# Attention in an encoder block: V as the stationary operand with two heads side by side in the array's columns, the two local score groups interleaved on row halves, and no transposes of the mixed heads

## The reference

```
# local heads: 8 query heads of 64, 2 kv groups of 4 heads; query block of 128
s = q @ k.T * 64**-0.5 - slope[h] * |distance|     # keys: 16 meta + blocks n-1, n, n+1
m = max(max(s), sink[h]); p = exp(s - m)
y_a = (p / (sum(p) + exp(sink[h] - m))) @ v
# latent (MLA) heads: 8 heads, q and k of 96, v of 64, all 1040 keys
y_b = softmax(q @ k.T * 96**-0.5) @ v
h = x + concat(y_a, y_b) @ w_out
# then RMSNorm and a top-4-of-32 mixture of experts, added to h
```

## Time and profile before

| | |
|---|---|
| median of 3 runs | 2566.9 us (2562.52 to 2570.47) |
| the profiled execution's own time | 2575.11 us |
| its span in the trace | 2573.4 us |
| mean granted TensorE clock | 0.945 of full speed |
| attend, by the trace | about 252.5 to 885 us |

### The profile page before, as it was taken

The page is one execution under the profiler, slowest core; times in us unless marked ns, Lnnn a source line. Parts: engine busy times, 40 slices in busy tenths (PEclk is TensorE's granted clock), DMA queues, the critical chain, the costliest instruction groups (busy, mean ns, idle before and its releaser), DMA issues.

```text
span 2573.4 us, 36097 instructions
## 1 busy us (share of the span) xinstructions
PE 2425.0 (94%) x15012; PEld 1858.4 (72%) x15012; DVE 749.6 (29%) x2121; ACT 452.7 (18%) x1120; POOL 224.3 (9%) x251
## 2 busy tenths in 40 slices
PE   7998999999999774799999999999999999999996
PEld 3554767777777561777888788788787878787875
DVE  4555433543444255111122122122121212121211
ACT  2333332332333130101111111111111111111110
POOL 0000000000000005011121111121100000000000
PEclk9999898998999755899999999999999999999998
DMA  3000300000000222976777788788889888888873
GB/s 144 24 2 21 125 17 1 17 17 17 17 17 9 66 93 82 386 256 225 264 271 279 264 290 292 277 292 298 321 305 326 306 325 305 326 304 325 304 267 83
DMA packets 199046, 486.41 MB, mean 189 GB/s; under 512 B 15137, under 2 KB 17313, under 8 KB 198417
## 3 DMA queue, kind: packets, MB, share of 16 engines
q1 hardware_dynamic: 176864, 442.85, 46.5%
q0 software_dynamic: 16320, 38.27, 6.4%
q10 hardware_dynamic: 5696, 2.95, 0.4%
HBM read 452.51 MB, written 38.21 MB: 191 GB/s over the span
## 4 chain that ended last, share of the span: by engine, by line
PE 59%; DMA 1%; POOL 0%; issue 0%; POOLq 0%; ACT 0%; ACTq 0%
PE gu_bank L1677 37%; PE ya_bank L1691 17%; PE yb_bank L1704 2%; PE xa_bank L1647 1%; PE xb_bank L1655 0%; DMA x_rows<-ffn_rows,tab 0%; DMA tab_b<-slot_table 0%; POOL x_rows L1445 0%; POOL sums L1488 0%; ACT y_rows L1562 0%; POOLq L1468 0%; POOL tab_b L1452 0%; ACTq L1580 0%; POOLq L1448 0%; POOLq L1452 0%
## 5 line engine op out<-in xcount | busy, mean ns | idle before, releaser
L1677 PEld LDWEIGHTS gu_bank<-xT,ring 128*128 128x128 f32 x8192 | 965.1, 191 | 15.5 <-issue 15.5
L1677 PE MATMUL gu_bank<-xT,ring 128*128 128x128 f32 (+10 forms) x8192 | 968.5, 281 | 0.7 <-issue 0.7
L1691 PE MATMUL ya_bank<-ring,hidden 128*128 128x512 f32 x1024 | 446.2, 594 | 0.0
L1605 DVE TENSOR_SCALAR g_in<-gu_bank,bias_cur 128x128 f32<-128x128 f32 (+10 forms) x256 | 91.9, 359 | 1192.2 <-PE gu_bank L1677 1192.2
L1691 PEld LDWEIGHTS ya_bank<-ring,hidden 128*128 128x128 f32 x1024 | 192.0, 190 | 230.0 <-issue 225.5
L1556 ACT ACTIVATE sig<-g_in 128x128 f32<-128x128 f32 (+10 forms) x256 | 81.3, 317 | 875.8 <-DVE g_in L1605 875.8
L484 PE MATMUL proj_bank<-w_in_sb,normT 128*128 128x512 f32 (+3 forms) x432 | 149.8, 501 | 9.8 <-DVE w_in_sb L369 8.9
L867 PE MATMUL score_bank<-mla_kT,mla_qT 96*128 96x512 f32 x256 | 140.9, 678 | 0.0
L1488 POOL DMA_INDIRECT sums<-y_rows,tab x32 | 51.7, 1616 | 963.1 <-ACT y_rows L1562 963.1
L484 PEld LDWEIGHTS proj_bank<-w_in_sb,normT 128*128 128x128 f32 (+1 forms) x432 | 70.9, 182 | 78.4 <-issue 65.6
L907 PE MATMUL mla_bank<-mla_v,probsT 128*128 128x64 f32 x1024 | 121.4, 272 | 0.0
(11 more groups left out here) (240 smaller groups left out, 1863.4 us busy)
## 6 DMA issues: line engine op xcount, KB each, us to landing
ring<-in_w_gate SPq DMA_DIRECT2D x64, 2048.0 KB, 12.3
ring<-in_w_up SPq DMA_DIRECT2D x64, 2048.0 KB, 10.6
ring<-in_w_down SPq DMA_DIRECT2D x64, 2048.0 KB, 14.2
w_in_sb<-in_w_in SPq DMA_DIRECT2D x8, 592.0 KB, 8.8
xt<-in_x SPq DMA_DIRECT2D x8, 512.0 KB, 3.9
resid<-in_x SPq DMA_DIRECT2D x8, 512.0 KB, 3.6
w_out_sb<-in_w_out SPq DMA_DIRECT2D x1, 4096.0 KB, 16.9
residual<-resid SPq DMA_DIRECT2D x8, 512.0 KB, 2.6
```

The costliest lines, as they stand in the source:

```text
L1605: v.tensor_scalar(g_in[:, f % 2, 0:width], gu_bank[:, f % 2, 0:width], bias_cur[:, f:f + 1], LIMIT, ALU.add, ALU.min).then_inc(g_ready, 1)
L1677: last = nc.tensor.matmul(gu_bank[:, f % 2, i * 256:i * 256 + width], w[:, k, c * P:(c + 1) * P], xT[:, k, 0:width], start=(k == 0), stop= ...
L1691: last = nc.tensor.matmul(ya_bank[:, h, :], hidden[:, k, 0:P], w[:, k % 4, h * 512:(h + 1) * 512], start=(k == 0), stop=(k == FC - 1))
```

## The change

- **Values, MLA heads.** V is now stationary (64 columns) and `probsT` moving (128 columns). The output has head dimensions on the partitions: head 2p on partitions 0 to 63 and head 2p+1 on 64 to 127 of `mla_bank`, and the code alternates between the two (`mla_values`). It works on a pair of heads at once, half of the key blocks in one step and half in the next. `probsT` gets four buffers.
- **Local heads.** A unit is now a pair of heads, one of each kv group: `UNITS = 12`. Its scores alternate between array rows 0 to 63 and 64 to 127 and go to separate banks; its values (`swa_values`) are paired in the columns as above. Its transposes are split between `act_bank` and `dve_bank`.
- **Normalisation.** The output is already transposed, so `mixed` and its eight transposes go away. To scale along the free dimension, TensorE spreads each head's inverse sum over 64 partitions by a matmul with the identity (8 matmuls for MLA in step i = 10, 8 for local heads in step i = 1), ScalarE copies the bank to `inv_wide`, and VectorE multiplies it with the values' bank straight into `mixedT`. The output projection moves from step i = 5 to i = 3.
- **Meta values.** One matmul of 512 columns becomes four of 128.
- **DMAs.** `w_out` comes in three DMAs with its local half reordered. The rows past the end of `sums` are filled from `x` by one DMA instead of zeros by a memset and two.

```diff
@@ attend @@
-    UNITS = MLA_HEADS + SWA_HEADS
+    UNITS = MLA_HEADS + PAIRS
+    EVENTS = MLA_HEADS // 2 + PAIRS
...
-        no_rows = m.sb("no_rows", [P, 2 * D])
-        probsT = m.sb("probsT", [P, 2, DC, P])
-        biased = m.sb("biased", [P, 2, BAND])
+        probsT = m.sb("probsT", [P, 4, DC, P])
+        biased = m.sb("biased", [P, 2, SWA_KV, BAND])
-        mixed = m.sb("mixed", [P, 2 * 512])
+        inv_wide = m.sb("inv_wide", [P, 512])
...
@@ gpsimd @@
-                nc.gpsimd.memset(no_rows[:], 0.0).then_inc(no_rows_set, 1)
-                pool.wait_ge(no_rows_set, 1)
-                for b in range(0, TRASH, 2 * P):
-                    pool.dma_start(io["acc"][SEQ + b:SEQ + b + 2 * P, :].rearrange("(p j) d -> p (j d)", p=P), no_rows[:])\
-                    .then_inc(y_zeroed, 16)
+                pool.dma_start(io["acc"][SEQ:SEQ + TRASH, :].rearrange("(p j) d -> p (j d)", p=P),
+                               io["x"][0, 0:TRASH, :].rearrange("(p j) d -> p (j d)", p=P)).then_inc(y_zeroed, 16)
@@ scalar @@
+                    if i == 10:
+                        if t >= 1:
                             act.wait_ge(swa_mixed, t)
+                        copy_T(("mla", t), inv_wide[:], act_bank[:]).then_inc(act_T_out, 1)
+                    if i == 1 and t >= 1:
+                        act.wait_ge(mla_mixed, t)
+                        copy_T(("swa", t - 1), inv_wide[:], act_bank[:]).then_inc(act_T_out, 1)
@@ vector @@
+                    if i == 1 and t >= 1:
+                        dve.wait_ge(sink_done, t)
+                        link(v.tensor_tensor(swa_inv[:], band_sum[:].rearrange("p (g j) -> p j g", j=PAIRS),
+                                             sink_exp[:].rearrange("p (g j) -> p j g", j=PAIRS), ALU.add))
+                        v.reciprocal(swa_inv[:], swa_inv[:]).then_inc(swa_inverse, 1)
...
+                    if i == 2 and t >= 1:
+                        dve.wait_ge(values_done, t * EVENTS)
+                        dve.wait_ge(act_T_out, at_act["swa", t - 1] + 1)
+                        v.tensor_tensor(mixedT[:, 0:4, :].rearrange("p k q -> p (k q)"), swa_bank[:], inv_wide[:], ALU.mult)\
+                            .then_inc(swa_mixed, 1)
@@ tensor: scores @@
-                        g, pair = divmod(i - MLA_HEADS, PAIRS)
-                        r = slice(g * HD, (g + 1) * HD)
                         for at, key, keys, _, _ in band_parts(t):
-                            last = nc.tensor.matmul(bank[:, at:at + keys], swa_qT[r, pair, cols(t)],
-                                                    swa_kT[r, key:key + keys], start=True, stop=True)
+                            for g in range(SWA_KV):
+                                r = slice(g * HD, (g + 1) * HD)
+                                last = nc.tensor.matmul(bank[:, g * 512 + at:g * 512 + at + keys],
+                                                        swa_qT[r, i - MLA_HEADS, cols(t)],
+                                                        swa_kT[r, key:key + keys], start=True, stop=True)
@@ tensor: values @@
-                        for k in range(DC):
-                            last = nc.tensor.matmul(mla_bank[:, i * VD:(i + 1) * VD], probsT[:, n % 2, k, :],
-                                                    mla_v[:, k, i, :], start=(i == 0 and k == 0), stop=False,
-                                                    skip_group_check=True)
+                    for k in range(4 * half, 4 * half + 4):
+                        for j in range(2):
+                            last = nc.tensor.matmul(mla_bank[j * VD:(j + 1) * VD, pair * P:(pair + 1) * P],
+                                                    mla_v[:, k, 2 * pair + j, :], probsT[:, (n - 1 + j) % 4, k, :],
+                                                    start=(pair == 0 and k == 0), stop=False, skip_group_check=True)
...
+                    for x, (_, _, keys, kt, slot) in enumerate(parts):
+                        for g in range(SWA_KV):
+                            last = nc.tensor.matmul(swa_bank[g * HD:(g + 1) * HD, pair * P:(pair + 1) * P],
                                                     swa_v[0:keys, kt, g * HD:(g + 1) * HD],
+                                                    probsT[0:keys, n % 4, 4 * g + slot, :],
                                                     start=(x == 0), stop=(x == len(parts) - 1))
@@ tensor: inverse sums, out @@
+                        pe.wait_ge(mla_inverse, t + 1)
+                        pe.wait_ge(act_T_out, at_act["mla", t])
+                        for h in range(MLA_HEADS):
+                            p, j = divmod(h, 2)
+                            last = nc.tensor.matmul(act_bank[j * VD:(j + 1) * VD, p * P:(p + 1) * P],
+                                                    mla_inv[:, h:h + 1].to_broadcast([P, VD]), ident[:],
+                                                    start=True, stop=True)
...
-                            for k in range(4):
-                                c = (c0 + k) * P
-                                last = nc.tensor.transpose(bank[:, k * P:(k + 1) * P], mixed[:, c:c + P], ident[:])
```

More of the change, by code:

```diff
@@ L620, in attend @@
         dve_own = m.sem("dve_own_a")
-        fills, act_T, dve_T = [], [], []
-        for n in range(TILES * UNITS + 8):
+        OUT = 3
+        STEPS = TILES * UNITS + OUT + 2
+        fills, act_T = [], []
+        for n in range(STEPS):
             t, i = divmod(n, UNITS)
@@ L777, in _ @@
                 take_meta(0)
-                for n in range(TILES * UNITS + 8):
+                for n in range(STEPS):
                     t, i = divmod(n, UNITS)
-                    if i == 6 and t >= 1:
+                    if i == OUT + 1 and t >= 1:
                         j = at_fill["out", t - 1]
@@ L897, in transpose_probs @@
-                    last.then_inc(dve_T_done, 1)
-                def values(n):
+                        if g == 1 and n:
+                            pe.wait_ge(dve_T_out, n)
+                        if i < MLA_HEADS:
+                            for k in range(4):
+                                last = nc.tensor.transpose(bank[:, k * P:(k + 1) * P],
+                                                           probs[:, n % 2, (4 * g + k) * P:(4 * g + k + 1) * P], ident[:])
+                        else:
+                            for c, _, keys, _, slot in band_parts(t):
+                                last = nc.tensor.transpose(bank[0:keys, slot * P:(slot + 1) * P],
+                                                           probs[:, n % 2, g * 512 + c:g * 512 + c + keys], ident[:])
@@ L900, in values, with mla_values @@
+                        last.then_inc(done, 1)
+                def mla_values(n, half):
                     t, i = divmod(n, UNITS)
-                    pe.wait_ge(dve_T_out, at_dve["unit", n] + 1)
-                    if i < MLA_HEADS:
+                    pair = i // 2
+                    if half == 0:
+                        pe.wait_ge(dve_T_out, n + 1)
                         pe.wait_ge(act_T_out, at_act["unit", n] + 1)
-                        if i == 0 and t >= 1:
+                        if pair == 0 and t >= 1:
@@ new lines, in mla_values, with swa_values @@
+                    if half:
+                        last.then_inc(values_done, 1)
+                def swa_values(n):
+                    t, i = divmod(n, UNITS)
+                    pair = i - MLA_HEADS
+                    pe.wait_ge(dve_T_out, n + 1)
+                    pe.wait_ge(act_T_out, at_act["unit", n] + 1)
+                    if pair == 0:
+                        pe.wait_ge(meta_read, min(t + 2, TILES))
+                    parts = band_parts(t)
+                    for x, (_, _, keys, kt, slot) in enumerate(parts):
+                        for g in range(SWA_KV):
+                            last = nc.tensor.matmul(swa_bank[g * HD:(g + 1) * HD, pair * P:(pair + 1) * P],
@@ L939, in _ @@
                             pe.wait_ge(v_meta_in, 16 * MLA_HEADS)
-                        nc.tensor.matmul(mla_bank[:], meta_pT[:], v_meta[:].rearrange("p h c -> p (h c)"),
-                                         start=False, stop=True, skip_group_check=True).then_inc(mla_done, 1)
-                    if i == 3 and t >= 1:
-                        pe.wait_ge(swa_mixed, t)
-                        pe.wait_ge(mla_mixed, t)
-                        for bank, out, done, key, c0 in ((act_bank, act_T_out, act_T_done, at_act["mixed", t - 1], 0),
-                                                         (dve_bank, dve_T_out, dve_T_done, at_dve["mixed", t - 1], 4)):
-                            pe.wait_ge(out, key)
-                            for k in range(4):
-                                c = (c0 + k) * P
-                                last = nc.tensor.transpose(bank[:, k * P:(k + 1) * P], mixed[:, c:c + P], ident[:])
-                            last.then_inc(done, 1)
@@ L952, in _ @@
-                    if i == 5 and t >= 1:
```

(16 more changed lines are left out.)

196 lines of the change are left out of this document (94 added, 102 removed).

## The result

| | before | changed |
|---|---|---|
| median | 2566.24 us (4 runs, 2562.52 to 2570.47) | 2452.87 us (4 runs, 2445.94 to 2468.14) |
| ratio | | 0.9562, 95% interval 0.9528 to 0.9595 |
| profiled span | 2573.4 us | 2456.8 us |
| attend, first DMA to last store of `h` | 252.5 to 885.2: 632.7 us | 251.3 to 771.0: 519.7 us |

The kernel is 113 us faster. The gain stands in attend: 113.0 us of it there, out of 116.6 between the two spans.

A forecast was written before the change was run, and what follows sets the result against it. TensorE's queue was taken to bound attend; terms summed to -75.4 us at full clock, about -80 at a granted clock of 0.92, giving 2487 us on the median's scale, with a range of 2463 to 2532.

The forecast's parts named there:

- A: MLA values: 64 blocks of 1.73 us become 64 half pairs of 1.16, saving 36.5 us.
- B: Local values: 60 groups of eight at 1.07 us become 30 blocks of 1.16, saving 29.4 us.
- Rival 3: Paired values: column halves don't overlap with weight loads of the same rows; +48 us, 2615 us, chance 0.07.
- C: Local scores: two row halves load and stream at once, saving 29.7 us, with little confidence.
- Rival 1: Local scores: row halves don't overlap, loads go one after the other; 2519 us, chance 0.30.
- D: Attend's mix: 64 transposes go (-7.0 us), sixteen blocks spreading inverse sums come (+18.6); net +11.6 us.
- E: MLA steps: new TensorE waits, 0.7 to 0.75 us a tile at i = 2 and 0.2 at i = 1; +7.6 us.
- F: Local steps: ScalarE and VectorE keep up, costing nothing while TensorE stays above about 3.1 us a step.
- G: Start of attend: the earlier fill of `sums`, also reading 2 MB, runs beside the constants' load; +1 us.
- The sum at full clock: Attend: all terms added at full clock, -75.4 us, before stretching by the granted clock to about -80.
- rival 2's opposite: Attend's clock: paired columns keep more of the array at work, saving half of 41 us; 2465 us, chance 0.05.
- The loss side of rival 2: Attend, chiefly local steps: lower clock or dependency chain takes gain back, leaving 20 to 40 us; some 2535 us, chance 0.12.

The follow-up runs named there:

- columns_in_turn: Changed kernel with paired values doing all key blocks of one head, then of the other, instead of alternating column halves; 2513.43 us, ratio to before 0.9775.
- fill_late: Changed kernel with GpSimd waiting for the bias and sink constants before the 2 MB fill of `sums`; 2452.82 us, ratio to before 0.9577, attend 512.1 us.
- before_again: The kernel before, unaltered, traced a second time; 2558.27 us (one run), attend 614.3 us.
- before_wide_local: The kernel before with 128 streaming columns in local values only, where the neighbouring 64 exist; 2532.36 us, ratio to before 0.9888, attend 606.6 us.
- before_wide_both: The kernel before with 128 streaming columns in MLA and local values, MLA sums altered so only attend counts; attend 598.9 us, total 2524.69 us.
- rows_in_turn: Changed kernel with local scores doing all parts of one kv group, then the other, instead of alternating row halves; 2473.24 us, ratio to before 0.9614.

## Why the prediction was right and wrong

**The bound** was read rightly: TensorE's queue set attend before and sets it now.

**A and B, the column pairs: right.** 1.11 and 1.26 us a block, forecast 1.16. A came to 64 x (1.73 - 1.11) = 39.7 (forecast 36.5), B to 64.2 - 30 x 1.26 = 26.4 (forecast 29.4); that the two misses cancel is luck. Rival 3 fell: the halves overlap with their loads hidden, also at 128 columns, and columns_in_turn shows that it is the alternation that does it. The Trainium skill's rule from TensorE: Matmul & The Clock Gate, The mechanism, that a load overlaps a running matmul only in another row group, disagrees with the trace here too: by it the block of 16 over the same 128 rows would have taken 2.03 us.

**C, the row halves: right**, though no row had shown them. A block is 1.00 us; 59.4 - 30.0 = 29.4 saved, forecast 29.7. The prediction took this by analogy from columns, with little confidence, so the close number is partly luck. Rival 1 fell. What I did not know is that about 0.43 us a block would have come from joining two heads in one step, in either order.

**D: right.** The spreading takes 1.02 us a block (1.16 in the sum), which makes the net +9.3 instead of +11.6.

**E: right in place, too dear.** 0.56 instead of 0.7 at i = 2, and no wait for the inverse sums at i = 1. **F: wrong in part.** It put the waits in local steps at nothing. TensorE waits 0.25 us a tile for the last MLA head's exponentials, in the first local step, and 0.34 before the meta transpose:

```profile
489.19 0.33 PE L960 MATMUL act_bank<-ident_sb,meta_p 128*128 128x128 f32 x1 [0.34 <-ACT probsT L736]
```

Together TensorE waits 10.0 us for ScalarE behind the start, where E and F had 7.6.

**G: the size was off.** VectorE began 4.9 us later, not 1: the fill of `sums` took the DMA engines from `band_bias`, as fill_late shows.

**The sum at full clock holds.** A mean clock of 0.93 over the 610 us from 275 to 885 means that some 85 us of them ran at half speed, and cost at most half of that, 42.7. Without it attend before would have taken about 590.0 us, an estimate; the same working on before_again, with 51 us, gives 588.8. Against 519.7 that is 70.3 us saved, where the sum said 75.4, and 71.5 with G corrected. With every term as measured above it is 39.7 + 26.4 + 29.4 - 9.3 - 10.0 - 4.9 = 71.3.

**The step that failed** is the one that the prediction put as "Attention ran at a granted clock of 0.92, and the TensorE terms stretch with it: about -80". It carried the lower clock over to the changed kernel as if it belonged to the chip. The clock of attend behind its start was 1.00 there instead of 0.93. The lower clock belonged to the instruction stream: before_wide_local and before_wide_both keep the kernel before and stream 128 columns in its values, and the stretches go. The changed kernel streams 128 columns too, by making `probsT` the streaming operand, and gained up to 42.7 us on top of the sum (24 if before_again is taken as the kernel before). That this is what cured the changed kernel is argued from those runs; no run gave it back its narrow values. rows_in_turn and columns_in_turn only show that neither alternation by itself keeps the clock up. The prediction had this case, as rival 2's opposite, "paired columns keep more of the array at work", with a chance of 0.05 and half of the 41 us that the earlier trace rows show. Both were too small: the two stretches quoted make 41 of about 85 us, and that the values' pace is 0.108 where 64 columns stream in 0.054 follows from the first part, which did not ask what this does to the clock. The loss side of rival 2, which worried about the local stretch, had 0.12 and nothing came of it.

## What to carry to other kernels

Where rows at 1.2 GHz stand in a stretch in which TensorE is always busy, ask which of its groups are paced by weight loads and stream little behind them; to make the larger operand the streaming one can bring back the clock as well as the time. Take a second trace before pricing such stretches: here they came to 85 us in one and 51 in the other. Outputs of 64 partitions or contractions of 64 rows are worth pairing, and most of it comes only if the code alternates between the halves. Before a bulk DMA is moved forward or turned from SBUF to DRAM as its source, look who waits for the small loads beside it.

## What the runs showed of the hardware

- A kernel can get faster by streaming more: before_wide_local, 0.9888 (0.9838 to 0.9939), with the clock in attend at 0.97 instead of 0.92 to 0.95.
- TensorE can fall to 1.2 GHz while it is busy without a gap: 3.40 of 3.40 us busy from 506.2 us on, 24.00 of 24.00 from 390 us on the earlier trace rows.
- Matmuls of different halves overlap even where the code takes one half after the other: 16 local scores in 1.55 us where two separate blocks of eight took 1.98, and up to seven on record as running in one 0.1 us window.
- A part with 16 rows inside column pairs is dear when the halves are taken in turn: the local block took 2.31 us, against 1.17 with alternation.
- A DMA of 2 MB from DRAM to DRAM, started 0.6 us behind one of 1.6 MB, made that land after 12.2 us. It was 6.8 beside the fill from SBUF, which started 2.6 us behind, and 6.1 with the fill held back until it had landed. Whether the source or the earlier start does it was not told apart.
